# Second mixer's query and key products in the feed-forward's form, with copies through ScalarE

## What is computed

```python
proj = rmsnorm(x, mix_norm) @ w_in
qa, ka, va, qb, kb, vb = split(proj)          # 512 columns each
oa = diff_attention(qa, ka, va, lam, bias)    # 4 heads of two maps
ob = dilated_attention(qb, kb, vb, bias)      # 8 heads
x = x + concat(rmsnorm(oa) * gain, ob) @ w_out
```

## Time and profile before

| what | us |
|---|---|
| median of 3 runs (lowest to highest) | 950.36 (950.25 to 950.77) |
| the profiled execution | 950.8 |
| its span, first to last instruction | 949.0 |
| TensorE busy | 941.4 |
| VectorE busy | 692.5 |
| ScalarE busy | 521.7 |

### The profile page before, as it was taken

How to read it: one execution, slowest core, us unless ns; L and a number is a source line. 1 busy time by engine, 2 the same in 40 slices (tenths; PEclk the granted TensorE clock), 3 DMA queues, 4 the chain that set the end, 5 groups by cost and what they waited for, 6 DMA issues and landing times.

```text
span 949.0 us, 13943 instructions
## 1 busy us (share of the span) xinstructions
PE 941.4 (99%) x5616; PEld 813.7 (86%) x5616; DVE 692.5 (73%) x997; ACT 521.7 (55%) x659; POOL 69.6 (7%) x148
## 2 busy tenths in 40 slices
PE   9999999999999999999999999999999999999997
PEld 9988888798888888888888888889898888888886
DVE  6788568887858777788885757578778677566675
ACT  6676767555355556555654435356446455354554
POOL 1020227141200000000000000000002000000000
PEclk9999999999999999999999999999999999999999
DMA  9844554333565455655464554653534446646441
GB/s 358 329 151 164 177 182 173 134 129 138 181 237 188 165 212 178 222 178 202 153 219 180 183 218 172 223 181 134 192 128 169 155 137 219 222 144 222 166 178 45
DMA packets 25808, 174.07 MB, mean 183 GB/s; under 512 B 3216, under 2 KB 3472, under 8 KB 5776
## 3 DMA queue, kind: packets, MB, share of 16 engines
q1 hardware_dynamic: 25168, 170.17, 50.1%
q10 hardware_dynamic: 576, 3.01, 0.9%
HBM read 172.12 MB, written 1.05 MB: 182 GB/s over the span
## 4 chain that ended last, share of the span: by engine, by line
PE 99%; DVE 0%; ACT 0%; issue 0%; POOL 0%; ACTq 0%; POOLq 0%
PE ps L410 52%; PE ps L417 25%; PE ps L421 13%; PE ps L523 1%; PE ps L622 1%; PE ps L749 1%; PE ps L780 1%; PE ps L764 1%; PE ps L815 1%; PE ps L674 1%; PE ps L613 0%; PE ps L829 0%; PE ps L795 0%; PE ps L541 0%; PE ps L701 0%; PE ps L864 0%
## 5 line engine op out<-in xcount | busy, mean ns | idle before, releaser
L1581 DVE TENSOR_TENSOR Wl<-raw,Wh 128x2048 fp32r<-128x2048 f32 x151 | 345.6, 2291 | 35.2 <-ACT Wh L1092 34.5
L1092 ACT ACTIVATE Wh<-raw 128x2048 fp32r<-128x2048 f32 x154 | 294.2, 1912 | 39.9 <-PE ps L410 35.8
L417 PE MATMUL ps<-hT,Wh 128*128 128x512 f32 x1056 | 247.9, 390 | 0.0
L417 PEld LDWEIGHTS ps<-hT,Wh 128*128 128x128 f32 x1056 | 197.0, 188 | 40.3 <-issue 0.2
L410 PE MATMUL ps<-Wh,hT 128*128 128x512 f32 (+1 forms) x640 | 201.4, 387 | 0.0
L410 PEld LDWEIGHTS ps<-Wh,hT 128*128 128x128 f32 x640 | 118.3, 188 | 23.8 <-issue 1.3
L1424 ACT ACTIVATE Am<-ps 128x512 f32<-128x512 f32 x66 | 39.1, 592 | 178.8 <-PE ps L421 176.6
L421 PEld LDWEIGHTS ps<-hT,Wl 128*128 128x128 f32 x1056 | 132.4, 192 | 3.4
L421 PE MATMUL ps<-hT,Wl 128*128 128x256 f32 x1056 | 133.4, 283 | 0.0
L1666 DVE TENSOR_TENSOR PT<-ps,Am 128x256 f32<-128x256 f32 x132 | 49.7, 418 | 108.4 <-ACT Am L1424 108.2
L410 PE MATMUL ps<-Wh,yTh 128*128 128x512 f32 (+1 forms) x314 | 123.0, 392 | 0.0
(11 more groups left out here) (253 smaller groups left out, 815.1 us busy)
## 6 DMA issues: line engine op xcount, KB each, us to landing
raw<-in_units SPq DMA_DIRECT2D x154, 1024.0 KB, 4.8
FP<-in_bias ACTq DMA_DIRECT2D x1, 2048.0 KB, 11.5
FP<-in_first SPq DMA_DIRECT2D x2, 768.0 KB, 8.2
FP<-in_first SPq DMA_DIRECT2D x3, 384.0 KB, 4.8
raw<-in_units SPq DMA_DIRECT2D x2, 512.0 KB, 10.1
X<-in_x SPq DMA_DIRECT2D x1, 1024.0 KB, 17.0
Hn<-in_mem SPq DMA_DIRECT2D x1, 1024.0 KB, 9.4
XT<-in_mem_turned SPq DMA_DIRECT2D x1, 1024.0 KB, 11.4
```

The costliest lines, as they stand in the source:

```text
L417: pe.matmul(o, lh(k), hT_both(k), start=first and k == ks[0], stop=False)
L1092: act.activation(wh[j % NS][:, 0:n], raw[j % NR][:, 0:n], ACT.Copy).then_inc(w_hi, 1)
L1581: dve.tensor_tensor(wl[j % NS][:, 0:n], raw[j % NR][:, 0:n], wh[j % NS][:, 0:n].bitcast(F32), ALU.subtract).then_inc(w_lo, 1)
```

## The change

All four queries' and four keys' units take the feed-forward's form. `norm_pair` uses `wide` and `narrow`. `rows_out` becomes `crossed_rows`: each half m of a unit takes its own bank, waits for the high part only, does eight `wide`, waits for the low part, and does eight `narrow`. ScalarE copies every full bank (128x512) into SBUF (`keep_rows`), by turns into `Am` and `E1`, which empties the bank. A copy waits until VectorE has added the unit two before. VectorE's `join_rows` waits for both copies, adds their halves in SBUF (128x512 out) and scales the sum. The scores wait for the scaled rows by a semaphore of their own (`rows_made`). The copies and joins stand at these places:

```diff
 # TensorE
+            def crossed_rows(key, banks, mid=None):
+                i = U[key]
+                for m in range(2):
+                    b = banks.take()
+                    t = take(key + (m,), b)
+                    if m == 0:
+                        pe.wait_ge(w_hi, i + 1)
+                    wide(t, weight_left(i, 256, m * 128)[0], EIGHT, True)
+                    if m == 0:
+                        weights(i)
+                    narrow(t, weight_left(i, 256, m * 128)[1], EIGHT, True).then_inc(ps_full[b], 1)
+                    if m == 0 and mid:
+                        mid()
+                unit_end[i] = full(key + (1,))
...
-                        ins = three(ts[j][m][:, 0:256], weight_left(U[keys[j]], 256, m * 128), right(hT_at), ks, first, last)
+                        wide(ts[j][m], weight_left(U[keys[j]], 256, m * 128)[0], ks, first)
+                        ins = narrow(ts[j][m], weight_left(U[keys[j]], 256, m * 128)[1], ks, last)
...
+                if i % 4 == 0:
+                    pe.wait_ge(rows_made, i // 2 + 2)
...
 # ScalarE
+            def keep_rows(key, m):
+                n = rows_no(key)
+                act.wait_ge(*full(key + (m,)))
+                if n >= 2:
+                    act.wait_ge(rows_joined, n - 1)
+                act.activation(kept(key)[:, m * 512:m * 512 + 512], bank[at[key + (m,)][0]][:, :],
+                               ACT.Copy).then_inc(*emptied(key + (m,)))
...
-                hi_to(U[key] + 3)
+                hi_to(U[key] + 2)
...
             act.wait_ge(rstd_made, 4)
+            keep_rows(("qa", 0), 0)
+            keep_rows(("qa", 0), 1)
+            hi_to(U["qa", 0] + 3)
+            keep_rows(("ka", 0), 0)
+            keep_rows(("ka", 0), 1)
+            keep_rows(("qa", 1), 0)
             begin(("qa", 1))
+            keep_rows(("qa", 1), 1)
             exps(1, 0)
             exps(1, 1)
             begin(("ka", 1))
+            keep_rows(("ka", 1), 0)
+            keep_rows(("ka", 1), 1)
             exps(1, 2)
...
             exps(1, 5)
+            keep_rows(("qb", 0), 0)
             begin(("qb", 0))
             exps(1, 6)
             exps(1, 7)
+            keep_rows(("qb", 0), 1)
+            keep_rows(("kb", 0), 0)
             begin(("kb", 0))
+            keep_rows(("kb", 0), 1)
+            keep_rows(("qb", 1), 0)
             begin(("qb", 1))
             exps(1, 8)
             exps(1, 9)
+            keep_rows(("qb", 1), 1)
             act.wait_ge(*free(("do", 3)))
             act.activation(E0, OA[:, :], ACT.Square).then_inc(oa_sq, 1)
+            keep_rows(("kb", 1), 0)
             begin(("kb", 1))
             exps(1, 10)
             exps(1, 11)
+            keep_rows(("kb", 1), 1)
...
 # VectorE
+            def join_rows(dst, key, scale=None):
+                d, r = v3(dst), kept(key).rearrange("p (m s n) -> p m s n", m=2, s=2)
+                for m in range(2):
+                    dve.wait_ge(*free(key + (m,)))
+                dve.tensor_tensor(d, r[:, :, 0, :], r[:, :, 1, :], ALU.add).then_inc(rows_joined, 1)
+                dve.wait_ge(rows_joined, rows_no(key) + 1)
+                if scale is None:
+                    ins = dve.tensor_tensor(d, d, by_token(2), ALU.mult)
...
-            pair_scaled(QA[:, 0:512], ("qa", 0), -0.125)
-            pair_scaled(KA[:, 0:512], ("ka", 0))
+            join_rows(QA[:, 0:512], ("qa", 0), -0.125)
+            lo_to(U["qa", 0] + 3)
+            join_rows(KA[:, 0:512], ("ka", 0))
...
             begin(("qa", 1))
-            rows_scaled(QA[:, 512:1024], ("qa", 1), -0.125)
+            join_rows(QA[:, 512:1024], ("qa", 1), -0.125)
             guards(1, 0)
```

More of the change, by code:

```diff
@@ L204, in build @@
         sq_made = sem("sq_made")
+        rows_joined, rows_made = sem("rows_joined"), sem("rows_made")
         a_seq, v_seq, p_seq = sem("a_seq"), sem("v_seq"), sem("p_seq")
@@ L349, in crossed_out, with rows_no, kept @@
             return Am[:, n % 2 * 512:n % 2 * 512 + 512]
+        def rows_no(key):
+            return "ab".index(key[0][1]) * 4 + key[1] * 2 + "qk".index(key[0][0])
+        def kept(key):
+            return (Am, E1)[rows_no(key) % 2]
         def yT_at(k):
@@ L1037, in pe_program @@
             norm_pair(("qa", 0), ("ka", 0), 3)
-            rows_out(("qa", 1), W)
+            crossed_rows(("qa", 1), W)
             step(1, 0)
-            rows_out(("ka", 1), W)
+            crossed_rows(("ka", 1), W)
             step(1, 2)
             toks_halves("va", W, {(0, 0): lambda: step(1, None, 1), (1, 0): lambda: step(1, 4, 3)})
-            rows_out(("qb", 0), W, mid=lambda: step(1, 6, None, [1, 3]))
+            crossed_rows(("qb", 0), W, mid=lambda: step(1, 6, None, [1, 3]))
             step(1, None, 5)
-            rows_out(("kb", 0), W, mid=lambda: step(1, None, None, [5]))
+            crossed_rows(("kb", 0), W, mid=lambda: step(1, None, None, [5]))
             step(1, None, 7)
-            rows_out(("qb", 1), W, mid=lambda: step(1, 8, None, [7]))
-            rows_out(("kb", 1), W, mid=lambda: (turns(1, 8), step(1, 10)))
+            crossed_rows(("qb", 1), W, mid=lambda: step(1, 8, None, [7]))
+            crossed_rows(("kb", 1), W, mid=lambda: (turns(1, 8), step(1, 10)))
             step(1, None, 9)
@@ L1649, in norm_pair @@
                 spread_out(k)
-            def pair_scaled(dst, key, scale=None):
-                dve.wait_ge(*full(key + (1,)))
+            def join_rows(dst, key, scale=None):
+                d, r = v3(dst), kept(key).rearrange("p (m s n) -> p m s n", m=2, s=2)
                 for m in range(2):
[L1654 to L1659, removed]
+                    dve.wait_ge(*free(key + (m,)))
[3 more added lines that the diff above has]
+                    ins = dve.tensor_tensor(d, d, by_token(2), ALU.mult)
+                else:
+                    ins = dve.scalar_tensor_tensor(out=d, in0=d, scalar=scale, in1=by_token(2), op0=ALU.mult, op1=ALU.mult)
+                ins.then_inc(rows_made, 1)
             def up_sums(dst, key):
@@ L2185, in dve_program @@
             combine(0)
-            rows_scaled(KA[:, 512:1024], ("ka", 1))
+            join_rows(KA[:, 512:1024], ("ka", 1))
             guards(1, 2)
@@ L2201, in dve_program @@
             diff_out(1)
-            rows_scaled(QB[:, 0:512], ("qb", 0), -0.125)
+            join_rows(QB[:, 0:512], ("qb", 0), -0.125)
             copies(1, 5)
@@ L2206, in dve_program @@
             begin(("kb", 0))
-            rows_scaled(K[:, 0:512], ("kb", 0))
+            join_rows(K[:, 0:512], ("kb", 0))
             copies(1, 7)
@@ L2213, in dve_program @@
             shares(1, 8)
-            rows_scaled(QB[:, 512:1024], ("qb", 1), -0.125)
+            join_rows(QB[:, 512:1024], ("qb", 1), -0.125)
             dve.wait_ge(oa_sq, 1)
@@ L2222, in dve_program @@
             shares(1, 10)
-            rows_scaled(K[:, 512:1024], ("kb", 1))
+            join_rows(K[:, 512:1024], ("kb", 1))
             begin(("kb", 1))
```

## The result

The changed kernel takes 957.84 us (median of 6 runs, 956.06 to 958.2), the kernel before 950.29 (6 runs on the same chip): a ratio of 1.0073 [1.0064, 1.0083], 7.55 us slower. The profiled execution took 957.6 us for a span of 955.8, so 6.8 us more span than before. That is the forecast direction, 1.1 us above the forecast time and inside its range; but the measured time has two terms in it that my sum lacked (one I had priced at almost nothing, one I had not seen), and the sum's main term was too large.

What follows compares the result with a forecast made beforehand. TensorE, busy 99% of the span, was taken as the bound. 8.4 us more waiting less 1.6 to 1.8 us of products gave +6.5 us; 6.3 us was set on 950.4: 956.7 us, range 953.4 to 959.2.

Steps and rivals of the forecast that it cites:

- the sum's main term: TensorE's added waits in the second mixer: 9.2 us against 0.8 before, so 8.4 us more.
- the walk: Four engines' lists of the second mixer laid out in order with measured durations and hand-overs: +6.5 us.
- Rival 1: In the second mixer VectorE and ScalarE find the time, TensorE waits nowhere and keeps 1.6 us: 948.8 us, chance 0.06.
- the point that I said decides it: First turn: for a gain, ScalarE's cast of (va,0) must come before its wait for the half of (qa,1).
- a clock under 1.00 in a stretch: Sign of a wrong forecast: TensorE's granted clock below 1.00 (2.4 GHz) in a stretch of the mixer.
- transposes of map 9: Fourth turn: TensorE waits 1.2 us near 720 for VectorE's shares of map 9.
- TensorE's saving: Query and key units: each takes 5.56 us instead of 5.76, 0.20 less; eight units save 1.6 us.
- The bound for losses at each change of bank: Upper bound on TensorE: two more losses of 0.09 us in each unit, 16 x 0.09 = 1.4 us.
- transposes of map 3: Second turn: TensorE waits 2.7 us from 684.0 for VectorE's combination of head 1.
- each instruction starting when its engine is free: Rule for laying out the four engines: an instruction starts once its engine is free and its semaphores are up.
- a rival priced at 13.5 us: TensorE's clock falls to 1.2 GHz after each of five waits, 5 x 2.7 = 13.5 us: 970 us, chance 0.03.
- The scores' wait at map 12: Fifth turn: VectorE's rows of (kb,1) last to 724.3, and TensorE waits 0.4 us at the scores.

Runs made afterwards that it cites:

- the reordered kernel: Changed kernel with ScalarE's and VectorE's lists in another order and GpSimd's scaling waiting for the rows of (kb,1): 949.45 us, 0.9990.
- the two reordered kernels: Changed kernel with reordered ScalarE and VectorE lists and GpSimd's wait: 949.45 us with 512-column products, 950.45 us with each split into two of 256.
- the second experiment: Changed kernel with GpSimd's scaling of OA waiting until VectorE has scaled the rows of (kb,1): 956.32 us, 1.0058.
- products of 256: Changed kernel with each 512-column product of the eight units split into two of 256 columns: 958.47 us, 1.0082.
- filler: Changed kernel with nine overwritten products of 512 columns filling TensorE's wait before the transposes of map 3: 956.25 us, 1.0061.
- cast first: Changed kernel with ScalarE's cast of (va,0) before the copy of the first half of (qa,1): 955.60 us, 1.0055.
- no additions: Changed kernel without VectorE's eight additions, scaling only the first half of each sum: 953.32 us, 1.0032.
- reordered, GpSimd free: Changed kernel with only ScalarE's and VectorE's lists in another order, without GpSimd's wait: 951.32 us, 1.0008.

## Why the prediction was right, and where its sum was not

**Direction and mechanism: right.** Waits came at five of the places that the walk named, with the releasers that it named, and at the others there was next to none. That TensorE's waits make the loss, and that the order of the lists makes the waits, was shown by the runs: the cast ahead of the copy takes the first wait away, the whole order takes all of them. It was the right thing to lay out four lists of instructions rather than to count room: both engines had the room for the work, as the reordered kernel shows, and the change lost all the same. Rival 1 (the engines find the time) was wrong for this order and right for another; the point that I said decides it, the place of that cast, was the first step of the repair. But one of my own signs of being wrong was seen as well, "a clock under 1.00 in a stretch", and the forecast for the transposes of map 9 (1.2 us near 720) found no wait there.

**TensorE's saving: right for a unit, a little too high in the sum.** 5.56 us a unit was forecast, 5.58 came; the eight units give 1.4 us by their rows and 1.0 between the two reordered kernels, where the sum had 1.6. The bound for losses at each change of bank (16 x 0.09 us) was not needed in full: waits 6.8, clock 1.4, less the units' 1.4, make 6.8 us, and the mixer's stage is 7.4 us longer (its output products start at 748.49 instead of 741.67, and its first transposes 0.6 us earlier). 0.6 us lie in pieces too small to name.

**The walk's waits: places right, sizes too high.** TensorE's waits, forecast and measured from start to start: values' first product 1.3 and 0.8, transposes of map 3 2.7 and 2.2, values of map 5 1.3 and 0.8, transposes of map 9 1.2 and none, of map 11 1.8 and 1.2. All are some 0.5 us too high or more, and the step that failed, for the larger part, is "each instruction starting when its engine is free": I let the next start at the recorded end of the one before. The traces have it start earlier where it waits for nothing. The cast of 1.92 us at 657.29 is followed by the next instruction at 659.10, after 1.81; the low part at 725.52 of 2.28 by the copy at 727.72, after 2.20; two copies of 0.60 take 1.09. The walk loses 0.08 to 0.11 us at each such place. The profile of before has it too: there the low part at 717.47 of 2.28 us is followed at 719.67. Over the first two turns that makes 0.3 us a turn and not the whole 0.5: the walk is behind the trace by 0.56 us where the copy of ("qa",1)'s first half starts (663.2 against 662.64) and by 1.15 where the combination of head 1 ends (686.6 against 685.45). What it was behind before that is not explained here. The same two walks with starts in place of ends give, as an estimate whose steps are not shown here, +4.8 us in all, where 4.1 was measured with the two other terms away; they still have 0.7 us at map 9.

**The clock: a rival priced at 13.5 us with a chance of 0.03, and it came once, for 1.4 us.** The step that failed is "after each of five waits": the fall was taken as all or nothing. In the trace it came behind one wait of five, for seven products.

**GpSimd: not in the sum at all.** The edit was costed by each engine's own durations. "VectorE has no room" from 712 to 731 was seen, but I didn't ask what GpSimd's 6.81 us in that row lie beside. The scores' wait at map 12 was forecast at 0.4 us and was 1.8; the second experiment puts 1.5 us on it. Before, the long low part stood just ahead of GpSimd's instruction; after, the scaling stands just behind it. And the scaling itself is another kind of instruction now: before it read PSUM, after it reads two operands in SBUF, the kind that GpSimd's instruction takes turns with in these traces.

So the 7.55 us are 4.1 of turns (net) and 3.35 of clock and GpSimd, to 0.1 us; the forecast's 6.3 was one term too large standing in for three. That the time came within 1.1 us is luck to that extent: the turns alone were 2.2 us too high, and two terms that the sum lacked made up for it. Below it, the prices taken for the parts held: ScalarE's copies 0.60 us (0.59 forecast), the additions 0.69, the first guard at 668.71 (669.45 forecast, before 667.40), the cast of ("va",0) at 663.13 (663.8 forecast).

**Open.** What decides whether the clock falls, and why no wait came at map 9. And the six runs of the changed kernel lie at 956.06 to 956.08 and at 957.6 to 958.2, with nothing between. The distance is near the clock's term, but the two shorter runs have a mean clock of 0.996, as low as the others', so it is hardly that they were spared the fall; only the run of 957.6 has a trace.

## What to carry to other kernels

In a kernel with hand-written lists for engines that serve one another, work is priced by its place: with the old product size the same 16 copies and 8 additions cost 8.0 us in one order (958.47 against 950.48), and in another, with GpSimd's wait, none that could be measured (1.0001), at like busy shares. Walk the lists with start-to-start spacings, put what waits for late products behind what others wait for, and look at what runs on the engine that shares something with the one you move. A long wait that starts to show on TensorE can cost more than itself, as the one of 2.2 us did here; look at the clock in windows of one us behind it.

## What the runs showed of the hardware

**GpSimd and VectorE in turn.** Where VectorE's instruction reads two operands in SBUF, the second to start waits out the first in every trace here: GpSimd's 128x1024 multiplication ends some 1.77 us after VectorE's and shows 2.23, 2.35, 3.82 and 3.94 as it stands (1.90 where it started first); a 128x512 multiplication of VectorE shows 0.69 or 2.27, a low part 2.28 or 3.99. VectorE's copies from PSUM and its guards take their usual time beside it: with GpSimd late, a copy of 0.55 us at 726.12 and a guard of 0.28 at 726.58 lie within its 3.82 us from 724.14 on. A duration three times the usual in one instance of a group is hidden in the group's mean: it has to be looked for in the timeline.

**The clock fell after some waits of 2 us and not after others.** The longest gaps from start to start, the usual pitch included:

| kernel | longest gaps, us | clock |
|---|---|---|
| changed | 2.5 at 683, 2.0 at 724 | fell behind the first alone |
| products of 256 | 2.5 at 684, 1.9 at 725 | fell in the first alone, 0.3 us before its end |
| GpSimd late | 2.5 at 683 | fell behind it |
| filler | 2.0 at 722 | fell behind it |
| cast first | 2.2 at 683, 1.95 at 722 | 1.00 |
| no additions | 1.8 at 683, 1.5 at 725 | 1.00 |
| reordered, GpSimd free | 2.2 at 722 | 1.00 |

The 2.0 us gap of the filler's trace brought a fall, one of 2.2 us in two others did not. One and the same kernel shows both, too: with GpSimd late, one run has a mean clock of 0.999 and takes 954.55 us, the other three have 0.997 and take 956.06 to 956.71. The length alone doesn't decide, and no run here tells what does.

**The next instruction starts before the recorded end of the last,** by 0.08 us behind VectorE's low part and 0.11 behind ScalarE's cast. It does so where it waits for nothing: the scaling that waits for its own addition starts 0.04 us after the addition's recorded end (723.29, 723.33). So a recorded time is somewhat more than what an instruction costs its engine, unless the next one needs its result.
